# Chunk-band attention of one layer rearranged: two heads at a time on the halves of TensorE, plain transposes, and the query projection between the head pairs

## What is computed

```
q = (u @ w_q)                                   # 512 x 1024, 16 heads of 64
s = q_h @ k_h.T * 64**-0.5 + bias               # own chunk of 64 and the 8 before it
s = where(valid, s, -1e30)
p = softmax(s);  o_h = p @ v_h
mix = o @ w_o
```

## Time and profile before

| | |
|---|---|
| median of three runs | 2488.91 us (2487.29 to 2496.09) |
| the profiled execution | 2493.09 us, span 2491.1 us |
| TensorE matmul busy | 2284.4 us, 92% of the span |
| VectorE busy | 1389.3 us, 56% |
| ScalarE busy | 763.6 us, 31% |
| GpSimd busy | 420.5 us, 17% |
| query projection to the first matmul of the output projection | 1018.0 to 1187.04 us of the span |

### The profile page before, as it was taken

One profiled execution on the slowest core, in us unless ns is written; L12 is line 12 of the kernel. 1 busy time (PEld: TensorE's weight loads), 2 busy tenths in 40 slices (PEclk: granted clock), 3 DMA queues, 4 the chain that ended last, 5 costly groups with the idle time before them and its releaser, 6 DMA issues.

```text
span 2491.1 us, 25699 instructions
## 1 busy us (share of the span) xinstructions
PE 2284.4 (92%) x10168; PEld 1828.2 (73%) x10168; DVE 1389.3 (56%) x1822; ACT 763.6 (31%) x977; POOL 420.5 (17%) x272
## 2 busy tenths in 40 slices
PE   8989999979999979999899999889798876999996
PEld 6778788757888868766688888667466664888885
DVE  3467766556777773355444444563634555655556
ACT  1342333322222232355332222344123232322221
POOL 0000000069989833000000000000410000000000
PEclk9999999989999989999899999989889887999998
DMA  5333231225555524210222222222012221222220
GB/s 199 143 135 119 86 117 68 68 103 207 180 188 184 180 90 161 93 43 26 68 102 88 98 102 90 81 68 85 0 68 75 103 76 51 92 94 102 96 90 34
DMA packets 39646, 252.67 MB, mean 101 GB/s; under 512 B 4563, under 2 KB 4755, under 8 KB 11048
## 3 DMA queue, kind: packets, MB, share of 16 engines
q1 hardware_dynamic: 33176, 234.11, 26.7%
q0 software_dynamic: 3008, 10.63, 1.4%
q10 hardware_dynamic: 3344, 6.29, 0.7%
HBM read 244.73 MB, written 6.29 MB: 101 GB/s over the span
## 4 chain that ended last, share of the span: by engine, by line
PE 83%; DVE 9%; issue 3%; POOL 2%; ACT 2%; DMA 1%; SPq 0%; ACTq 0%; DVEq 0%; POOLq 0%
PE bank L634 23%; PE bank L636 22%; PE bank L635 22%; PE bank L677 2%; PE bank L839 2%; PE bank L941 2%; PE bank L951 1%; PE bank L929 1%; DVE w_lo L1543 1%; DVE scr L1573 1%; PE bank L759 1%; PE bank L753 1%; POOL raw L549 1%; PE bank L1020 1%; DVE scr L1611 1%
## 5 line engine op out<-in xcount | busy, mean ns | idle before, releaser
L634 PE MATMUL bank<-u_hi,w_hi 128*128 128x512 f32 x1772 | 712.9, 402 | 48.4 <-DVE u_lo L1605 11.2
L636 PE MATMUL bank<-u_hi,w_lo 128*128 128x512 f32 x1772 | 699.9, 395 | 0.0
L635 PE MATMUL bank<-u_lo,w_hi 128*128 128x512 f32 x1772 | 699.6, 395 | 0.0
L1543 DVE TENSOR_TENSOR w_lo<-raw,w_hi 128x2048 fp32r<-128x2048 f32 x165 | 437.6, 2652 | 311.6 <-ACT w_hi L1114 311.4
L634 PEld LDWEIGHTS bank<-u_hi,w_hi 128*128 128x128 f32 x1772 | 339.6, 192 | 130.6 <-issue 49.3
L1114 ACT ACTIVATE w_hi<-raw 128x2048 fp32r<-128x2048 f32 x165 | 314.9, 1909 | 362.8 <-PE bank L636 305.8
L636 PEld LDWEIGHTS bank<-u_hi,w_lo 128*128 128x128 f32 x1772 | 338.4, 191 | 72.5
L635 PEld LDWEIGHTS bank<-u_lo,w_hi 128*128 128x128 f32 x1772 | 339.7, 192 | 67.6 <-issue 0.2
L634 PE MATMUL bank<-g_hi,w_hi 128*128 128x512 f32 x708 | 282.1, 398 | 17.0 <-DVE w_lo L1543 12.6
L635 PE MATMUL bank<-g_lo,w_hi 128*128 128x512 f32 x708 | 279.1, 394 | 0.0
L636 PE MATMUL bank<-g_hi,w_lo 128*128 128x512 f32 x708 | 278.5, 393 | 0.0
(11 more groups left out here) (249 smaller groups left out, 2344.9 us busy)
## 6 DMA issues: line engine op xcount, KB each, us to landing
raw<-in_wts SPq DMA_DIRECT2D x221, 1024.0 KB, 4.9
spectra<-pool ACTq DMA_DIRECT2D x16, 256.0 KB, 2.0
pool<-in_rel POOLq DMA_DIRECT2D x16, 256.0 KB, 3.0
pool<-spectra POOLq DMA_DIRECT2D x16, 256.0 KB, 3.1
H<-in_x ACTq DMA_DIRECT2D x1, 2048.0 KB, 20.7
out<-H SPq DMA_DIRECT2D x1, 2048.0 KB, 7.1
pool<-in_window POOLq DMA_DIRECT2D x1, 1024.0 KB, 8.8
pool<-in_filt_w POOLq DMA_DIRECT2D x1, 512.0 KB, 5.9
```

The lines of the kernel that those rows point to most:

```text
L634: pe.matmul(out, lh, rh, start=start, stop=False, skip_group_check=True)
L635: pe.matmul(out, lh, rl, start=False, stop=False, skip_group_check=True)
L636: return pe.matmul(out, ll, rh, start=False, stop=stop, skip_group_check=True)
L1543: dve.tensor_tensor(w_lo[w % hi_ring][:, :], raw[W_STREAM[w] % raw_ring][:, :], w_hi[w % hi_ring][:, :].bitcast(F32), ALU.subtract).then_i ...
```

## The change

Heads are handled in pairs `g` (heads `2g` and `2g + 1`).

- `scores(g, j)` runs row block `j` of both heads one after the other: the even head on rows 0 to 63 into bank 2, the odd head on rows 64 to 127 into bank 3. `weighted(g)` alternates the two heads, whose outputs lie in the two column halves and in one bank.
- `turn(h, j)` is a plain transpose by `ident`. The inverse sums are multiplied into `b_s` on VectorE beforehand, in place, one multiplication for each row block (`normalise`); `b_dg` and its diagonals are gone. `b_s` has three buffers (the third in `macc`), `b_pt` two.
- Only slot 0 of the query projection is done ahead of the attention. `query_steps` cuts slots 1 to 3 in steps of 6 matmuls; four steps go with the scores of pair 0 and four with each of pairs 0 to 4. `out_steps` does the same for slot 0 of the output projection: four steps in pair 6, two in pair 7, two behind it. Slots of `qq` use banks 0 and 1 alone (`PLACE` and `BEFORE` replace `n % 4` and `n - 4`). The results of pairs 0 to 3 go to `g_hi` and `g_lo`, those of pairs 4 to 7 to `u_hi` and `u_lo`.
- TensorE's order in a pair: for each row block `turn(2g, j)`, `scores(g + 1, j)`, a step; then `turn(2g + 1, j)` for the four blocks; then `weighted(g)`.

```
-    out("qq", 8, "act", slots=[("qq", i) for i in range(4)])
-    out("wo1", 8, "dve", slots=[("wo1", i) for i in range(4)])
+    out("qq", 8, "act", slots=[("qq", i) for i in range(4)], banks=(0, 1))
+    out("wo1", 8, "dve", slots=[("wo1", i) for i in range(4)], banks=(0, 1, 2, 3))
...
-        b_s = [ar(1280), scr[:, 4:7, :].rearrange("p a b -> p (a b)")[:, 0:1280]]
-        b_pt = scr[:, 0:4, :]
-        b_mx = ar(8)
-        b_sm = ar(8)
-        b_rc = ar(8)
-        b_dg = view(ar(2 * TB * P), 2, TB, P)
+        b_s = [ar(1280), ar(1280), macc[:, :, :].rearrange("p a b -> p (a b)")[:, 0:1280]]
+        pt_row, pt_words = 384, 3 * 384 + SEQ
+        b_pt = [scr[:, :, :].rearrange("p a b -> p (a b)")[:, x * pt_words:(x + 1) * pt_words] for x in (0, 1)]
...
+        def pair_event(h, j):
+            return 8 * (h // 2) + 2 * j + h % 2
+        def o_ready(pc):
+            return (g_l, G_O + pc + 1) if pc < 4 else (u_l, U_O + pc - 3)
...
-            for i in range(4):
-                slot_std("qq", i, FIRST["qq"] + 2 * i, U_MIX1)
-            pe.wait_ge(free["act"], FREES[FIRST["qq"] + 7][1])
-            def scores(h):
-                for j in range(TB):
-                    if h:
-                        pe.wait_ge(at_sc, 4 * (h - 1) + j + 1)
-                    n = (j + 1) * P
+            def query_steps(i):
+                w, hi, lo = weights("qq", i)
+                banks = [claim(FIRST["qq"] + 2 * i + j) for j in range(2)]
+                for k in range(KC):
+                    wait_u(U_MIX1 + k + 1)
+                    for j in range(2):
+                        c = k * 256 + j * P
+                        mm = three(banks[j][:, :], hi[:, c:c + P], lo[:, c:c + P], u_hi[:, k, :], u_lo[:, k, :],
+                                   k == 0, k == KC - 1)
+                        if k == KC - 1:
+                            complete(mm, FIRST["qq"] + 2 * i + j, w if j else None)
+                    yield
+            def out_steps(i):
+                w, hi, lo = weights("wo1", i)
+                banks = [claim(FIRST["wo1"] + 2 * i + j) for j in range(2)]
+                for k in range(KC):
+                    pe.wait_ge(*o_ready(k))
+                    oh, ol = (x[:, (G_O + k) % NG, :] for x in (g_hi, g_lo)) if k < 4 else (x[:, k, :] for x in (u_hi, u_lo))
+                    for j in range(2):
+                        c = k * 256 + j * P
+                        mm = three(banks[j][:, :], hi[:, c:c + P], lo[:, c:c + P], oh, ol, k == 0, k == KC - 1)
+                        if k == KC - 1:
+                            complete(mm, FIRST["wo1"] + 2 * i + j, w if j else None)
+                    yield
+            def scores(g, j):
+                if j == 0:
+                    pe.wait_ge(*free_of(FIRST["qq"] + g))
+                n = (j + 1) * P
+                for h in (2 * g, 2 * g + 1):
+                    e = pair_event(h, j)
+                    if e >= 2:
+                        pe.wait_ge(at_sc, e - 1)
                     r = (h % 2) * HD
-                    pe.matmul(bank[j][:, 0:n], b_q[r:r + HD, h // 2, j * P:n], b_k[r:r + HD, h // 2, 0:n],
+                    pe.matmul(bank[2 + h % 2][:, 0:n], b_q[r:r + HD, g, j * P:n], b_k[r:r + HD, g, 0:n],
                               start=True, stop=True).then_inc(at_s, 1)
-            def turn(h):
-                pe.wait_ge(at_p, h + 1)
-                for j in range(TB):
-                    n = 4 * h + j
-                    if n >= 2:
-                        pe.wait_ge(at_pt, n - 1)
-                    for i in range(j + 1):
-                        c = b_off[j] + i * P
-                        mm = pe.matmul(bank[4 + j % 2][:, i * P:(i + 1) * P], b_s[h % 2][:, c:c + P], b_dg[:, h % 2, j, :],
-                                       start=True, stop=True)
-                    mm.then_inc(at_tr, 1)
-            def weighted(h):
-                pe.wait_ge(at_pt, 4 * (h + 1))
-                r = (h % 2) * HD
-                if h % 2 == 0 and h >= 4:
-                    pe.wait_ge(u_l, U_O + h // 2 - 1)
+            def turn(h, j):
+                n = 4 * h + j
+                pe.wait_ge(at_p, n + 1)
+                if n >= 2:
+                    pe.wait_ge(at_pt, n - 1)
+                for i in range(j + 1):
+                    c = b_off[j] + i * P
+                    mm = pe.transpose(bank[4 + j % 2][:, i * P:(i + 1) * P], b_s[h % 3][:, c:c + P], ident[:, :])
+                mm.then_inc(at_tr, 1)
+            def weighted(g):
+                pe.wait_ge(at_pt, 8 * (g + 1))
+                if g >= 2:
+                    pe.wait_ge(*o_ready(g - 2))
                 for i in range(TB):
-                    mm = pe.matmul(bank[6 + h // 2 % 2][r:r + HD, i * P:SEQ], b_v[:, i, h * HD:(h + 1) * HD], b_pt[:, i, i * P:SEQ],
-                                   start=(i == 0), stop=(i == 3), skip_group_check=True)
+                    for x in (0, 1):
+                        h = 2 * g + x
+                        c = i * pt_row + i * P
+                        mm = pe.matmul(bank[6 + g % 2][x * HD:(x + 1) * HD, i * P:SEQ], b_v[:, i, h * HD:(h + 1) * HD],
+                                       b_pt[x][:, c:c + SEQ - i * P], start=(i == 0), stop=(i == 3), skip_group_check=True)
                 mm.then_inc(at_o, 1)
+            for step in query_steps(0):
+                pass
             pe.wait_ge(mod_col, NVMOD)
             pe.wait_ge(*released(NORM["kv"]))
-            scores(0)
-            scores(1)
-            for h in range(B_HEADS):
-                turn(h)
-                if h + 2 < B_HEADS:
-                    scores(h + 2)
-                weighted(h)
-            for i in range(4):
-                slot_std("wo1", i, FIRST["wo1"] + 2 * i, U_O)
+            pe.wait_ge(*free_of(FIRST["vv1"] + 3))
+            steps = query_steps(1)
+            for j in range(TB):
+                scores(0, j)
+                next(steps)
+            for g in range(PAIRS):
+                if g in (1, 3):
+                    steps = query_steps(2 + g // 2)
+                if g == 6:
+                    steps = out_steps(0)
+                for j in range(TB):
+                    turn(2 * g, j)
+                    if g + 1 < PAIRS:
+                        scores(g + 1, j)
+                    if g < 5 or g == 6:
+                        next(steps)
+                if g in (0, 2, 4):
+                    assert next(steps, None) is None
+                for j in range(TB):
+                    turn(2 * g + 1, j)
+                    if g == 7 and j < 2:
+                        next(steps)
+                weighted(g)
+            for step in steps:
+                pass
+            pe.wait_ge(at_sc, 4 * B_HEADS)
+            for i in range(1, 4):
+                for step in out_steps(i):
...
+            def queries(i):
+                for c in (2 * i, 2 * i + 1):
+                    evacuate(FIRST["qq"] + c, b_q[:, c, :])
+            def exponentials(g, j):
+                for h in (2 * g, 2 * g + 1):
+                    x = 4 * (h % 4) + j
+                    act.wait_ge(at_mx, pair_event(h, j) + 1)
+                    s = b_s[h % 3][:, b_off[j]:b_off[j] + (j + 1) * P]
+                    act.activation(s, s, ACT.Exp, bias=b_mx[:, x:x + 1], accum_out=b_sm[:, x:x + 1]).then_inc(at_e, 1)
+            def turned_weights(h, j):
+                act.wait_ge(at_tr, 4 * h + j + 1)
+                if h >= 2:
+                    act.wait_ge(at_o, h // 2)
+                a = (h % 2) * pt_words + j * P
+                rows = scr[:, :, :].rearrange("p a b -> p (a b)")[:, a:a + (j + 1) * pt_row]
+                src = bank[4 + j % 2][:, 0:(j + 1) * P].rearrange("p (i q) -> p i q", q=P)
+                act.activation(rows.rearrange("p (i r) -> p i r", r=pt_row)[:, :, 0:P], src, ACT.Copy).then_inc(at_pt, 1)
+            ahead("qq", 0)
+            queries(0)
+            ahead("qq", 1)
             for j in range(TB):
-                exponential(0, j)
-            for h in range(B_HEADS):
-                if h:
-                    act.wait_ge(at_o, h)
-                    if h % 2 == 0:
-                        pc = h // 2 - 1
-                        act.wait_ge(product, used("qq", 3))
-                        act.activation(u_hi[:, pc, :], bank[6 + pc % 2][:, :], ACT.Copy).then_inc(u_h, 1)
+                exponentials(0, j)
+            for g in range(PAIRS):
                 for j in range(TB):
-                    act.wait_ge(at_tr, 4 * h + j + 1)
-                    b = bank[4 + j % 2][:, 0:(j + 1) * P].rearrange("p (i q) -> p i q", q=P)
-                    act.activation(b_pt[:, 0:j + 1, j * P:(j + 1) * P], b, ACT.Copy).then_inc(at_pt, 1)
-                    if h + 1 < B_HEADS:
-                        exponential(h + 1, j)
-            act.wait_ge(at_o, B_HEADS)
-            act.activation(u_hi[:, 7, :], bank[7][:, :], ACT.Copy).then_inc(u_h, 1)
+                    turned_weights(2 * g, j)
```

(92 more changed lines are left out.)

66 lines of the change are left out of this document (27 added, 39 removed).

## The result

| | before | after |
|---|---|---|
| median of 5 runs | 2489.62 us (2487.29 to 2501.37) | 2511.56 us (2501.07 to 2514.68) |
| ratio | | 1.0061 (95% interval 1.0039 to 1.0082) |
| profiled span | 2491.1 us | 2506.9 us |
| end of query slot 0 to start of output slot 1 | 169.1 us | 182.2 us |

The changed kernel is 0.6% slower, by the ratio of all runs with its interval; the quotient of the two medians would be 1.0088. The page of the profile after, against the earlier trace rows: TensorE is busy for 21 us less, and the span is 16 us longer.

The account below looks back on a forecast made before the run. TensorE bounds the stretch before; after the change, waits through VectorE and ScalarE do. 160.0 us at full clock plus 19.5 for clock falls gives 179.5 against 169.1; 10.4 more on the 2488.9 median is 2499 us, range 2462 to 2522.

Parts of the forecast that it names:

- the forecast's own 2492 to 2506: Whole kernel: long waits and clock falls in most pairs give 2492 to 2506 us; chance 0.43.
- What bounds the kernel: Attention stretch: TensorE bounds it before, 118.55 of 120 us busy; after the change, waits between engines set the rounds.
- a sum of TensorE's savings: TensorE's work for a pair with steps, by totals: 13.4 us, which would promise a large gain.
- The round: One pair, from weighted sum to weighted sum, through TensorE, VectorE and ScalarE: 19.3 or 20.0 us with steps.
- the first half: TensorE's transposes, scores, three steps and breaks in a pair: even head's last scores end at 8.55 us, odd head's at 9.0.
- The clock: TensorE's clock falls in eight idle stretches: 2.0 us each plus 3.5 for last transposes, 19.5 us in all.
- The halves: Half-array matmuls on TensorE overlap in full: scores 3.52 us a pair instead of 4.70, weighted sum 2.48 instead of 4.60.
- Rival C: Half-array matmuls on TensorE do not overlap: 26 us on top of the stretch's 179.5, 2525 us; chance 0.15.
- Its other mechanism: Changes between full and half array drain TensorE, 0.3 us each, 19 us more over seven pairs; 0.04 of the 0.15.
- VectorE's products: Multiplying inverse sums into exponentials on VectorE: about 1.2 us a head, off the path, costed at nothing.
- Rival D: Waits shrink through odd-head copies before about 11 us in the round; cheaper TensorE work decides: 2445 to 2465 us; chance 0.17.

Follow-up runs that it names:

- Steps late: Changed kernel with the four projection steps of a pair moved behind all its scores: 2472.36 us, ratio 0.9889 to the kernel before.
- copies first: Changed kernel with ScalarE's evacuations and weight rounding behind the odd head's four copies, VectorE's w_lo behind the next normalisations: 2496.19 us, ratio 0.9996.
- gap filled: Changed kernel with four unused fp32 matmuls of 512 columns in each of TensorE's eight idle stretches: 2486.43 us, ratio 0.9962.
- the file order: Weighted sum by whole heads, even then odd, in the changed kernel with projection steps moved behind the scores: 2480.91 us, ratio 0.9950.
- transposes alone: Kernel before with only plain transposes and inverse sums multiplied in on VectorE; heads single, projections outside: 2493.21 us, ratio 0.9991.
- one step early: Changed kernel with steps behind scores and odd head's copies ahead of evacuations and rounding, but one step back behind row block 1's scores: 2468.42 us, ratio 0.9907.
- heads in file: Changed kernel with the weighted sum of the even head in one piece, then the odd head's: 2511.16 us, ratio 1.0045.

## Why the prediction held

The forecast was 2499 us, 10.4 more than before in the stretch; measured are 2511.56, and 13.1 us more in the profiled stretch. The total lies 12.6 us above the point: inside the range, but outside the forecast's own 2492 to 2506, to which I had given 0.43. That the total is in the range owes much to the range's width. What held is the mechanism, and the stretch to 2.7 us. Of the 15.8 us between the profiled spans, 13.1 are in the stretch; the rest is from parts that run the same program before and after. Point by point:

- **What bounds the kernel.** Right: a sum of TensorE's savings would have promised 13.4 us a pair. The waits gave rounds of 21.2 to 23.4 us where steps and scores are in them, and the chain went through ScalarE's order. Steps late, copies first and gap filled each changed one part of this chain, and each moved the time as the chain has it.
- **The round.** At full clock I had 20.0, 19.3 and 20.0 us for pairs 1 to 3, 19.3 for pair 4, 17.0, 18.1 and 9.5 for pairs 5 to 7. With the gaps filled the trace has 20.1, 19.3, 20.1, then 20.7, 16.9, 20.0 and 9.3. Pairs 4 and 6, which are longer, follow the two weighted sums that still took 3.8 us. Inside the round of pair 2 the steps fit as well: from the end of the sum (1080.91) the additions of row block 3 start at 9.0 us (forecast 8.85), the maxima are done at 12.4 (12.2), the exponentials at 13.9 (13.6), the evacuations at 14.9 (14.8), and the next sum starts at 16.9 (16.8).
- **A piece of luck in the first half.** Two of its terms were wrong and cancelled. The scores of a pair overlap in full, 2.35 us instead of the 3.52 that I took. The changes between transposes, scores and steps cost more: each row block has three of them, 0.13, 0.16 and 0.14 us in row block 3 (transposes from 1096.78 to 1097.31 against 0.40 of work, scores to 1098.37 against 0.90, the step to 1099.87 against 1.36) and 0.4 in row blocks 1 and 2. That is 1.6 to 1.7 us a round where I had 0.4.
- **The clock.** Right in kind and sign. I took 2.0 us for each of eight gaps and 3.5 for the last transposes, 19.5 in all. Filling the gaps gave back 18.7, with two sums still 1.4 us slow each. Adding these, I estimate the clock's cost at 21.5 us and the stretch at full clock at 160.7, so most of the 2.7 us by which the stretch was missed is the clock's. The odd head's transposes did not hold the clock in this kernel: at 1103.9 it fell, with three of the ten issued since 1099.8. The rule of the Trainium skill that I set beside it (TensorE: Matmul & The Clock Gate, Part 4: PE-mode transpose) is in line with that, though TensorE stood still for most of the gap, so the runs do not separate the two.
- **The halves.** The weighted sum was 2.37 us at full clock (forecast 2.48), and the file order 3.93. The scores did better than I had them, see below. Rival C is out. Its other mechanism, 0.3 us for each change of mode, is about twice what a change cost, but the cost is not absent, as I had read the rows: three changes a row block cost 0.4 us together. And I had overlooked a row. I wrote that the trace of before has no neighbours on different halves, but at its start `scores(0)` and `scores(1)` stand next to each other. Their sixteen passes are over in 4.33 us, two waits of TensorE for VectorE included, where 4.70 is the work in file, and from 1063.6 on four passes are in flight, where one head alone has two. So the overlap of row halves could have been known before; that of column halves could not.

```profile
1062.48 4.33 PE L929 MATMUL bank<-pool 64*128 64x128 f32 x16 [0.69 <-ACT pool L1125]
```

```profile
1063.60:1063.70 0.10, 0.10 (x4) 0.10 (x3) 1.00 0.00 0
```

- **VectorE's products.** 1.28 us a head, off the path in the changed kernel, as forecast. They were off it with transposes alone too, where they end 1.2 us before the transposes start (1111.15 and 1112.34).
- **Rival D** needed the odd head's copies early in the round. They stayed behind all else on ScalarE, as read from the order.

## What to carry to other kernels

When a stretch that one engine bounds is made cheaper, follow one round through all queues before summing the savings. Here 21 us of TensorE's busy time went, and the kernel got slower until the same steps were put where TensorE waited. Work moved between stages should stand where the engine would idle, not where it is already the one waited for. On TensorE a gap costs twice: its own length and, when the clock falls, 2.3 us or more after it (3.3 to 3.5 where a whole round could be compared); even useless matmuls in the gap were worth more than they cost.

## What the runs showed of the hardware that was not expected

- fp32 matmuls of two passes on the two row halves overlap in full, where I had expected three passes of four in file. The scores of row block 3 for both heads take 1.06 us from their start to the next step (1097.31 to 1098.37); in single file they took 1.8. Windows of 0.05 us show two passes from 1097.3 on and two more from 1097.8 on.
- The overlap shrinks when the two heads' waits are not over together. In the kernel with one step early, where each head's scores had to wait for its own addition on VectorE, the odd head's first pass started 0.5 us behind the even head's, and the same four passes took 1.59 us busy instead of 1.13.
- The same program behind the changed stretch took between 1284.8 and 1298.1 us. The longest and the shortest of these pieces (the changed kernel and heads in file) have the same 4909 matmuls, and VectorE and ScalarE are busy for the same time; TensorE is busy for 1164.5 and 1150.4 us. By the clock's records in the two traces the granted clock stands at 0.50 for 178 and 146 us of them. So the 13.3 us are TensorE's, at a lower granted clock. Why its falls land differently in each execution no run shows.

```profile
1208.80:2506.90 1298.10, 1164.45 (x4909) 928.90 (x4907) 685.56 (x845) 377.83 (x413) 44.90 (x82) 0.93 0.23 79
```

```profile
1221.20:2506.00 1284.80, 1150.44 (x4909) 920.09 (x4907) 685.54 (x845) 377.84 (x413) 44.93 (x82) 0.94 0.23 80
```
